# Product keys in one block, and four changes to what TensorE does between stages, in a two-block transformer kernel

## The reference, cut to what matters

```python
# first layer, index of attention b: which keys each query may see
logits = einsum('bqhd,bkd->bqhk', qii, k_idx) * (IDX_DIM ** -0.5)
score = einsum('bqh,bqhk->bqk', wi, relu(logits))
_, sel = lax.top_k(score, top_k)                      # then softmax over these keys

# first layer, experts
out = out + jnp.matmul(silu(h @ w_gate[e]) * (h @ w_up[e]), w_down[e]) * combine[:, e:e + 1]

# second layer, product keys: 16 of 128 x 128 experts for each of 8 heads
s1, i1 = lax.top_k(sc[:, :, 0], 16); s2, i2 = lax.top_k(sc[:, :, 1], 16)
top_s, pos = lax.top_k(s1[..., :, None] + s2[..., None, :], 16)
idx, gate = ..., softmax(top_s)
act = gelu(einsum('chkd,cd->chk', u[ic], hc))
out = einsum('chk,chkd->cd', gate * act, v[ic])       # u, v: 16384 x 1024 each
```

## Time and profile before

| | us |
|---|---|
| median of 3 runs | 3173.82 |
| fastest, slowest of them | 3164.05, 3178.97 |
| the profiled execution's own time | 3160.44 |
| its span, first to last instruction | 3158.6 |
| TensorE busy | 2945.9 |
| VectorE busy | 2003.4 |
| ScalarE busy | 1299.2 |
| GpSimd busy | 412.2 |
| mean granted TensorE clock | 0.954 |

### The profile page before, as it was taken

One profiled execution on the slowest core, in us unless ns is written; L12 is line 12 of the kernel. 1 busy time (PEld: TensorE's weight loads), 2 busy tenths in 40 slices (PEclk: granted clock), 3 DMA queues, 4 the chain that ended last, 5 costly groups with the idle time before them and its releaser, 6 DMA issues. The chain is left out here.

```text
span 3158.6 us, 35850 instructions
## 1 busy us (share of the span) xinstructions
PE 2945.9 (93%) x13585; PEld 2349.4 (74%) x13585; DVE 2003.4 (63%) x3251; ACT 1299.2 (41%) x2103; POOL 412.2 (13%) x293
## 2 busy tenths in 40 slices
PE   7999998899997998889799899999999979999998
PEld 6756786687885455747466678999999977787887
DVE  4574433687885146534523268889797867888886
ACT  4335422476774123424321143346666642323331
POOL 0000000100010000000000000021112323445442
PEclk9999999899998999997699999999999999999999
DMA  4120063476766110210022132477777988999996
GB/s 162 42 72 11 28 173 128 167 277 255 301 257 234 40 54 27 81 55 21 1 85 94 57 143 96 149 250 272 260 256 276 341 338 307 380 386 383 378 386 235
DMA packets 160459, 589.09 MB, mean 187 GB/s; under 512 B 15264, under 2 KB 87584, under 8 KB 132000
## 3 DMA queue, kind: packets, MB, share of 16 engines
q1 hardware_dynamic: 100384, 423.16, 36.7%
q0 software_dynamic: 41472, 138.45, 11.7%
q10 hardware_dynamic: 18432, 25.17, 2.2%
HBM read 558.39 MB, written 66.09 MB: 198 GB/s over the span
## 5 line engine op out<-in xcount | busy, mean ns | idle before, releaser
L2116 POOL DMA_INDIRECT RG<-in_un,EI x128 | 181.1, 1415 | 1460.6 <-DVE EI L2354 1047.2
L2597 PE MATMUL bank<-VH,GL 128*128 128x512 f32 x768 | 302.5, 394 | 28.4 <-PEq L2445 24.4
L2599 PE MATMUL bank<-VH,GH 128*128 128x512 f32 x768 | 300.7, 392 | 0.0
L2116 POOL DMA_INDIRECT RG<-in_vn,EI x128 | 188.4, 1472 | 277.0 <-DVE X L2130 261.7
L2597 PEld LDWEIGHTS bank<-VH,GL 128*128 128x128 f32 x768 | 144.5, 188 | 64.9 <-issue 31.7
L2130 DVE SCALAR_TENSOR_TENSOR X<-RG,DG,X 128x1024 f32<-128x1024 f32 x128 | 164.2, 1283 | 43.0 <-DMA RG<-in_vn,EI 39.4
L2127 DVE CUSTOM_DVE_ANT_0 RG<-RG,HR 128x1024 f32<-128x1024 f32 x128 | 156.5, 1222 | 36.6 <-DMA RG<-in_un,EI 35.9
L2100 PE MATMUL bank<-HTl,UH1r 128*128 128x384 f32 x512 | 173.8, 339 | 0.0
L2101 PE MATMUL bank<-HTh,UH1r 128*128 128x384 f32 x512 | 173.6, 339 | 0.0
L2100 PE MATMUL bank<-HTl,UH0r 128*128 128x384 f32 x512 | 172.8, 338 | 0.0
L2101 PE MATMUL bank<-HTh,UH0r 128*128 128x384 f32 x512 | 172.8, 337 | 0.0
(11 more groups left out here) (588 smaller groups left out, 7476.5 us busy)
## 6 DMA issues: line engine op xcount, KB each, us to landing
UR<-in_u SPq DMA_DIRECT2D x64, 1024.0 KB
VR<-in_vn SPq DMA_DIRECT2D x32, 2048.0 KB, 9.6
UP<-in_wup SPq DMA_DIRECT2D x22, 2048.0 KB, 7.7
DN<-in_wdn SPq DMA_DIRECT2D x32, 1024.0 KB, 7.6
W<-in_weights SPq DMA_DIRECT2D x20, 1536.0 KB, 6.5
W<-in_weights SPq DMA_DIRECT2D x14, 2048.0 KB, 8.2
aspill<-GA ACTq DMA_DIRECT2D x128, 192.0 KB
wspill<-VR SPq DMA_DIRECT2D x12, 2048.0 KB, 9.1
```

The lines of the kernel that those rows point to most:

```text
L2116: e.indirect_dma_start(RG[q % RR], None, d["un" if what == "u" else "vn"][:, :], off).then_inc(*row_in[q % RR].up(16))
L2597: e.matmul(bk, r(gl[:, a, t]), r(vh[:, a, :]), start=g == 0 and a == 0, stop=False)
L2599: i = e.matmul(bk, r(gh[:, a, t]), r(vh[:, a, :]), start=False, stop=g == 31 and a == 3)
```

## The change

It has five parts.

1. Index block: `upto` reaches 48 parts at step 39 and not 41, and TensorE ends the block with 2 `warm` matmuls and not 19.
2. Attention block: in each of the first 12 steps one `warm` matmul of 256 columns stands between attention b's piece and attention a's.
3. Router block: 8 `warm` matmuls of 512 columns stand ahead of the turns.
4. Expert block: the two builds of tile 3 stand one step earlier.
5. Product keys: the two blocks are one. The second's buffers are placed by address over buffers whose last use lies ahead. The groups go in the order 30, 31, 0 to 29 (`ORDER`). The gelu results of the last 8 `pe_first` stay in SBUF (in `AV[0]` and `AV[1]`), so groups 30 and 31 need no A from DRAM. `LAST` is 8. `FIRSTS` is 0.88 in 64 steps and 0.644 in 34; `TURNS` is 0.66 in 66 steps and 1.25 in 32, and `ROWS1` becomes 95.

```diff
-        def warm(e, times, bk):
+        def warm(e, times, bk, w=512):
-                e.matmul(bank[bk], ident, C[:, 0:512], start=True, stop=True)
+                e.matmul(bank[bk][:, 0:w], ident, C[:, 0:w], start=True, stop=True)
...
-                        warm(e, 19, 7)
+                        warm(e, 2, 7)
...
                             att_b.pe(e, step)
+                            if step < 12:
+                                warm(e, 1, 3, 256)
                             att_a.pe(e, step)
...
                     def _(e):
+                        warm(e, 8, 7)
                         norm.pe_turn(e)
...
+            ORDER = [30, 31] + list(range(30))
-            def load_a(e, g):
+            def load_a(e, k):
                 for n in range(4):
-                    e.wait_ge(*ga_done[n](16 * g + 16))
-                if g >= 2:
-                    e.wait_ge(*g_lo(g - 1))
-                e.dma_start(AV[g % 2], AD[g]).then_inc(*a_in[g % 2].up(16))
+                    e.wait_ge(*ga_done[n](16 * ORDER[k] + 16))
+                e.wait_ge(*g_lo(k - 1))
+                e.dma_start(AV[k % 2], AD[ORDER[k]]).then_inc(*a_in[k % 2].up(16))
...
             def dve_prod(e, g):
                 e.wait_ge(*ww_in[g % 2](16 * (g // 2) + 16))
-                e.wait_ge(*a_in[g % 2](16 * (g // 2) + 16))
+                if g >= 2:
+                    e.wait_ge(*a_in[g % 2](16 * (g // 2)))
+                else:
+                    e.wait_ge(*f_gelu(124 + 4 * g))
...
-                LAST = 4
+                LAST = 8
...
-                FIRSTS += [(128 - LAST - sum(FIRSTS)) / 98] * 98 + [1.0] * LAST
-                TURNS = [0.0] * (NQ + 14) + [0.5] * 14 + [0.7] * 66 + [1.4] * 32 + [0.5] * LAST
+                FIRSTS += [0.88] * 64
+                FIRSTS += [(128 - LAST - sum(FIRSTS)) / 34] * 34 + [1.0] * LAST
+                TURNS = [0.0] * (NQ + 14) + [0.5] * 14 + [0.66] * 66 + [1.25] * 32 + [0.5] * LAST
...
                     e.wait_ge(*f_mm(q + 1))
+                    if q >= 120:
+                        if q >= 124:
+                            e.wait_ge(*ga_done[q % 4](16 * 30))
+                        e.activation(AV[q // 4 - 30][:, q % 4, :], bank[place(q)][:, 0:NT3], ACT.Gelu).then_inc(*f_gelu.up(1))
+                        return
...
                     e.wait_ge(*v_lo(n + 1))
+                    if n == 0:
+                        e.wait_ge(*f_gelu(125))
+                        e.wait_ge(*o_copy(96))
+                    if n == 1:
+                        e.wait_ge(*f_gelu(126))
+                        e.wait_ge(*c_ia(3))
...
+                                if o == 92:
+                                    e.wait_ge(*ws_done[0](16 * NC // 2))
+                                    load_v(e, 0)
...
                         load_w(e, 0)
-                        load_a(e, 0)
-                        for g in range(2):
-                            load_v(e, g)
+                        load_v(e, 1)
+                        e.wait_ge(*f_mm(128))
+                        load_w(e, 1)
+                        for k in range(2, 32):
+                            load_w(e, k)
+                            load_a(e, k)
+                            load_v(e, k)
```

More of the change, by code:

```diff
@@ L599, in program @@
                 place = lambda u: 16 * (u // 8) + u % 8
-                upto = lambda step: 0 if step < FIRST else min(48, (step - FIRST + 1) * 9 // 4 + 1) if step < 28 else min(48, 39 + (step - 27) * 9 // 14)
+                upto = lambda step: 0 if step < FIRST else min(48, (step - FIRST + 1) * 9 // 4 + 1) if step < 28 else min(48, 39 + (step - 27) * 3 // 4)
                 def index_units(step):
@@ L1072, in program @@
         ENDED = sorted(range(NT + NO), key=lambda t: LAST_AT[t])
-        BUILDS = sorted(((max(FIRST_AT[t] - 3 + part, -2 + part), t, part) for t in range(NT + NO) for part in range(2)))
+        BUILDS = sorted(((max(FIRST_AT[t] - (4 if t == 3 else 3) + part, -2 + part), t, part) for t in range(NT + NO) for part in range(2)))
         BUILT = {(t, part): b for b, (_, t, part) in enumerate(BUILDS)}
@@ L2062, in program @@
             cu = c0.enter_context(ExitStack())
+            cu_at = nc.sbuf_base
             HH_, HL_ = (sb(n, [128, 8, 512], cu) for n in ("HTh", "HTl"))
@@ L2299, in program @@
                 GL[0] = nc.alloc_sbuf_tensor_at("GL0", [128, 4, NT3], F32, offset=OB_at)[:, :, :]
+                GA_at = nc.sbuf_base
                 GA = [sb(f"GA{n}", [128, NT3], cx) for n in range(4)]
+                AV[1] = nc.alloc_sbuf_tensor_at("AV1", [128, 4, NT3], F32, offset=GA_at)[:, :, :]
+                at = cu_at
+                for n in (1, 2):
+                    VH[n] = nc.alloc_sbuf_tensor_at(f"VH{n}", [128, 4, 512], F32, offset=at)[:, :, :]
+                    at += 8192
+                for name, where in (("GL1", GL), ("GH1", GH), ("WW1", WW)):
+                    where[1] = nc.alloc_sbuf_tensor_at(name, [128, 4, NT3], F32, offset=at)[:, :, :]
+                    at += 16 * NT3
+                assert at <= cu_at + 73728
                 WS = [VR[n][0].rearrange("p a n -> p (a n)").rearrange("p (i t) -> p i t", t=TW) for n in range(2)]
@@ L2443, in act_first, with pe_second @@
                     e.dma_start(AD[q // 4, :, q % 4, :], GA[q % 4]).then_inc(*ga_done[q % 4].up(16))
+                out_done = sem("out_done", True)
+                def pe_second(e, n):
+                    g, c = n // 2, span(n % 2, 512)
+                    gh, gl, vh, vl = GH[g % 2], GL[g % 2], VH[n % 3], VR[g % 2][1][:, :, c]
+                    e.wait_ge(*g_lo(g + 1))
+                    e.wait_ge(*v_lo(n + 1))
+                    if n == 0:
[4 more added lines that the diff above has]
+                        e.wait_ge(*c_ia(3))
+                    for tb in range(3):
+                        t, bk = span(tb), bank[2 * tb + n % 2]
+                        for a in range(4):
+                            e.matmul(bk, r(gl[:, a, t]), r(vh[:, a, :]), start=g == 0 and a == 0, stop=False)
+                            e.matmul(bk, r(gh[:, a, t]), r(vl[:, a, :]), start=False, stop=False)
+                            i = e.matmul(bk, r(gh[:, a, t]), r(vh[:, a, :]), start=False, stop=g == 31 and a == 3)
+                    i.then_inc(*y_mm.up(1))
+                later = lambda n: range(ROWS1 + n * (256 - ROWS1) // 60, min(256, ROWS1 + (n + 1) * (256 - ROWS1) // 60))
                 with nc.Block() as block:
@@ L2474, in _ @@
                         load_w(e, 0)
-                        load_a(e, 0)
-                        for g in range(2):
-                            load_v(e, g)
+                        load_v(e, 1)
[5 more added lines that the diff above has]
+                            load_v(e, k)
+                        e.wait_ge(*y_add(6))
+                        e.wait_ge(*r_used(256))
+                        e.dma_start(out.rearrange("(b p) n -> p b n", p=128), X).then_inc(out_done.sem, 16)
+                        e.wait_ge(out_done.sem, 16)
                     @block.gpsimd
@@ L2481, in _ @@
                         e.wait_ge(*r_ids(1))
-                        for q in range(ROWS1 + RR):
+                        for q in range(256):
                             pool_row(e, q)
@@ L2504, in _ @@
                                     pe_chosen(e, tb, part)
+                        for n in range(64):
+                            pe_second(e, n)
                     @block.scalar
@@ L2539, in _ @@
                             for q in rows(step):
+                                act_row(e, q)
+                        for n in range(64):
+                            if n % 2 and n < 63:
+                                act_gate(e, n // 2 + 1)
+                            if n < 63:
+                                act_v(e, n + 1)
+                            for q in later(n):
                                 act_row(e, q)
```

68 lines of the change are left out of this document (9 added, 59 removed).

## The result

Over 20 runs each the changed kernel takes 3148.63 us in the median (3125.15 to 3171.76), the kernel before 3175.46 (3156.63 to 3196.52): ratio 0.992, 95% interval 0.9896 to 0.9944. That is 26.8 us less, where 35.8 on the profiled execution and a median of 3138 were forecast. The profiled execution took 3125.15 (before: 3160.44), 35.3 less. Every ratio in this document leaves out runs over 1.5% above the fastest of the same kernel, which are four of e9's seven and one run of the kernel before (3219.93, beside e5 to e8); the medians have them in.

The account below looks back on a forecast made before the run. TensorE was taken as the bound, with DMA engines also full in the second product-key block; -5.4 - 3.5 - 8.2 - 18.7 = -35.8 on 3160.4 gives 3124.6, plus 13.4 to the median: 3138 us, range 3116 to 3160.

Parts of the forecast that it names:

- Index seam: End of the index block: VectorE ends it at 238.5, attention starts at 238.8 and not 250.91, -12.1 us.
- The 12 matmuls: Attention block's first 12 steps: the new 256-column matmuls cost 0.43 us each, in all +5.2 us, at the lower end 0.
- Clock at the attention's head: Attention's start: 2.9 us of TensorE idling lowers the clock for a while, +1.5 us, at most 9.
- rival 4: Head of the attention block: the clock is lost there, +9 us for +1.5, total 3146 us; chance 0.08.
- Router: Router block: 8 warm matmuls give a faster clock in turns and records, -3.5 us, from -6 to 0.
- Experts: Expert block: no step has two builds any more, -8.2 us, from -9 to -4.
- T: Product keys: the end of `pe_first(127)`, taken as +2 us; search steps -5 to 0, last 34 steps 0 to +8.
- Gap and start: Seam of the product keys: TensorE's 24.41 us gap goes, -24.4 us, with the first unit ready near T+1.5.
- Five more rows: Product keys' second part: 161 rows and not 156 at about 384 GB/s, +3.5 us.
- Rival 1: Product keys: DMA engines carry 375 and not 384 GB/s, 17 us and not 3.5, total 3152 us; chance 0.15.
- Rival 3: Product keys: the seam isn't closed, reads and writes take twice as long, 13 us come back, total 3151; chance 0.07.
- Rival 5: Product keys' second part: late rows in the four-buffer ring hold up V splits and TensorE, total 3199 us; chance 0.05.

Follow-up runs that it names:

- e9: The changed kernel with 5 warm matmuls, not 2, ending the index block and none in attention; median 3184.7 us, ratio 0.9904 to the kernel before.
- e5: The changed kernel run again unchanged; median 3166.6 us, ratio 0.9965 to the kernel before.
- e8: The changed kernel with 512 columns, not 256, in each of attention's 12 warm matmuls; median 3142.0 us, ratio 0.9899 to the kernel before.
- e7: The changed kernel with 5 warm matmuls, not 2, at the index block's end; median 3130.9 us, ratio 0.9871 to the kernel before.
- e3: Parts 1 to 4 of the change, with the product keys of the kernel before; median 3190.8 us, ratio 1.0042 to the kernel before.
- e4: The changed kernel without the 12 warm matmuls in attention; median 3154.4 us, ratio 0.9940 to the kernel before.
- e1: The kernel before run again unchanged; median 3177.5 us, ratio 1.0008.
- e2: Part 5 of the change alone, parts 1 to 4 as in the kernel before; median 3150.3 us, ratio 0.9926 to that kernel.
- e6: The changed kernel with index and attention blocks as before (parts 3 to 5 only); median 3153.4 us, ratio 0.9942 to the kernel before.
- e11: The changed kernel with 5 warm matmuls, not 2, and 0.74 and 1.08 rows a step, not 0.66 and 1.25; median 3113.2 us, ratio 0.9799 to before.
- e10: The changed kernel with 5 warm matmuls, not 2, and the old tables of the product keys' first part; median 3133.6 us, ratio 0.9871 to before.

## Why the prediction was right or wrong

- **Index seam: right**, -12.6 for -12.1. VectorE ended the block at 238.0.
- **The 12 matmuls: right on their price**, 4.6 us for 5.2 (e9 against e7).
- **Clock at the attention's head: wrong, and it is the step that failed.** The prediction took 1.5 for the 2.9 us of idling, from the earlier trace rows, and capped the loss with "the first 12 steps at half rate". Its rival 4, at +9, was the right mechanism with a half to a quarter of its price, and its own sign of being wrong, a head that runs at 0.5, came in e3, e4, e5 and e8. The row showed a clock that came back after 3.4 us, in a block with 512-column matmuls. In the attention block it stays away for 14 to 79 us behind that idle time: 8 us lost in e8, 19 in e5, 36 in e3, 35 in e4. The first trace of after lost nothing at the head (and 1.7 in 3.4 us at 1.2 GHz from 346.5 on, which make up its +6.3 with the 4.6). That the measured median still lies inside the forecast's own range is luck in part: it mixes runs near 3126, which lost nothing there if they are like the profiled one, with runs 20 to 45 us slower.
- **The baseline: not asked.** The before trace had no such stretch, three others with 19 `warm` ahead did (e1, e2, e6: 12 to 16 us lost, stretches of 27, 34 and 27 us). I added 13.4 us between profiled execution and median as if it were scatter; it is about what the attention block loses in most runs. That it is about the same size is argued from four traces, not shown run by run.
- **Router: wrong**, 0 for -3.5. The step said that a faster clock in the turns and records passes on. The 8 matmuls did not bring that clock: from the 29 turns' start to the records' end 8.9 us are at 1.2 GHz in before and 8.9 in after. Where more of it is, the part is longer (15.5 us in e5, 13.8 in e8).
- **Experts: right**, -7.7 for -8.2.
- **Second layer: +3.4, not forecast.** No instruction differs. Three traces without part 4 have 808.2 to 810.1 there, eleven with it 810.7 to 816.9. The clock's records have most of it: 153.3 us of the stage at 1.2 GHz in after and 148.0 before, 5.3 more, which at the 0.45 to 0.5 us lost for each is an estimate of 2.4 to 2.7 us. The longest stage, 816.9 (e11), has 165.9 us at 1.2 GHz; only e9 stands apart, 810.7 with 142.2. Why the clock differs there is open.
- **T: right in sum (-0.1 for +2), wrong in both terms.** Against the old tables with the same `LAST = 8` it is -11.8 (e10), outside the range given; so what else the change does there (4 more `pe_first` at the end, the V load, a block with a longer list) takes back some 12. Which of them wasn't tried. One sign: with the old tables TensorE waits 13.8 us for the selection in e10 and 6.0 in before, and at `LAST = 8` the search steps have fewer `pe_first` to fill them. What the DMA limit costs in the last 34 steps was put at 0 to 8. It was more, if late rows are put down to that limit: TensorE stands still for 16 of 110 us there and 2.2 in before, and moving 5 rows or so out of them won 17 (e11).
- **Gap and start: right**, first unit ready at T+1.3 for T+1.5. The +3 for unit 2 didn't come: TensorE is busy 21.8 of the 22 us from 2578 on.
- **Five more rows, +3.5: can't be told.** The second part took 535.3 with 156 rows (e10) and 536.3 to 544.5 in ten traces with 161 or 162; in the two-block kernels it took 537.8 to 549.3 (before, e3, e1). Rival 1 (375 GB/s) falls for the change: eleven traces with part 5 have 381 to 387 over 450 us. But 374 does happen: e1, the kernel before, had it, with a second part 11.5 us longer. Whether the rate or the clock came first there is open. Rival 3 falls: the seam is closed in all eleven traces. Rival 5 falls: TensorE's waits for V splits in after's second part are 3.3 us in all.

The median of 3148.6 was inside the range of 3116 to 3160. With e5's 12 runs it is 3161.7 over 32, against 3176.3 over 100 runs of the kernel before, e1's among them: 0.46% less, the edge of what can be told. "Same" was given 0.09 and deserved more.

The Trainium skill ("DMA: Bandwidth & Descriptors", Where 436 GB/s comes from) has 435 GB/s as the ceiling of the fabric. The trace of before comes near it at the program's start, 429 GB/s from 4 to 24 us. In its product keys the fullest 20 us have 413, and the second part of after holds 387 over 450 us, so for this stage the sums by 384 were nearer than a sum by 435:

```profile
4.00:24.00 20.00, 7.02 (x30) 6.17 (x31) 7.57 (x16) 9.88 (x16) 0.00 (x0) 1.00 1.02 429
...
2530.00:2550.00 20.00, 20.00 (x128) 20.00 (x128) 16.52 (x20) 13.19 (x28) 7.24 (x6) 1.00 1.01 413
```

## What to carry to other kernels

When work moves ahead of a stage of short, waiting matmuls, look at the granted clock of that stage in several executions, since one trace may have drawn the good case: here 3 us of idling at its door went with 19 or 35 us of loss in some executions, and 3 more dummy matmuls in that idle time, with 12 inside the first steps, cost nothing and took 36 us off the median on the same chip. Without the 12 the 3 did not do it (e9). When gathered rows land late in one stretch and the stretch ahead of it has DMA engines to spare, move gathers forward: here 5 of them won 17 us, beside the 11.8 of the tables that moved matmuls. Stop when the waits for the engine that uses them grow.

## What the hardware showed that I had not expected

- A stretch at 1.2 GHz in the attention block begins at the first matmul behind 2.88 us of idling (e4, e5, e8) or 2.2 us behind it (e3), or 4 to 5 us behind it after 0.3 us (e1, e2, e6), and lasts 14 to 79 us. Each us of it costs 0.45 to 0.46 us in six traces (35.5 for 78.5, 18.8 for 41, 12.4 for 27.3), and 0.58 in e8, where the 7.9 for 13.7 rests on an estimate.
- The shortest stretch, 13.7 us, is e8's, with 12 matmuls of 512 columns; with 256 columns it took 41 and 78.5 us. That the width did it isn't shown: these are single traces, and without any such matmuls it took 78.5 us in e4, and 27, 34 and 27 us behind 19 `warm`.
- The same program meets it in some executions and not in others. What decides that is open.
